# A two-layer block at 256 tokens: the first layer's work before its gathers put in another order

## The reference, cut to what matters

```python
# first layer: x is 1 x 256 x 1024
h = rmsnorm(x, norm1_gain)
aq, ak, av, mq, mk, mv, mi, mf, mo, gate_a, gate_m = split_columns(h @ w_in)
aq = partial_rope(rmsnorm(aq, q_norm_gain), positions)      # 16 heads of 64
ak = partial_rope(rmsnorm(ak, k_norm_gain), positions)      # 2 heads of 64
att_b = sliding_window_attention(aq, ak, av, sinks) @ w_branch_attn
hm = mlstm_chunkwise(mq, mk, mv, i_pre, f_pre)              # 8 heads, values of 128
hm = rmsnorm(hm, ml_out_norm_gain) * sigmoid(mo)
mixed = sigmoid(gate_a) * att_b + sigmoid(gate_m) * (hm @ w_branch_mlstm)
x = x + mixed @ w_out
x = x + peer_ffn(rmsnorm(x, norm2_gain), ...)
# peer_ffn: query projection, key scores, top 16 per head, 128 experts per token
# gathered by index (a down and an up row of 1024 each), softmax gate times gelu
# second layer, untouched: stick-breaking attention, HGRN2, a gated feed-forward
```

## Time and profile before

| | |
|---|---|
| median of 3 runs | 1484.26 us (1481.1 to 1486.63) |
| the profiled execution's own time | 1486.09 us |
| its span | 1484.3 us |
| PE busy | 1242.8 us (84%) |
| DVE busy | 725.6 us (49%) |
| ACT busy | 570.9 us (38%) |
| POOL busy | 819.7 us (55%) |
| mean granted TensorE clock | 0.93 of full speed |

### The profile page before, as it was taken

One profiled execution on the slowest core, in us unless ns is written; L12 is line 12 of the kernel. 1 busy time (PEld: TensorE's weight loads), 2 busy tenths in 40 slices (PEclk: granted clock), 3 DMA queues, 4 the chain that ended last, 5 costly groups with the idle time before them and its releaser, 6 DMA issues.

```text
span 1484.3 us, 16729 instructions
## 1 busy us (share of the span) xinstructions
PE 1242.8 (84%) x6460; PEld 902.9 (61%) x6460; DVE 725.6 (49%) x1423; ACT 570.9 (38%) x1220; POOL 819.7 (55%) x503
## 2 busy tenths in 40 slices
PE   5788879958668877787788878778899899999998
PEld 5787769858643333333333333333499899999997
DVE  3256310164567585858576766754467723311111
ACT  4345753122422232222233222322566546544442
POOL 5535437235565545544545454454286647698885
PEclk9889979979789989999989998999999999999999
DMA  6523323244079999999999999999754334455551
GB/s 193 171 96 100 99 86 113 68 132 142 29 304 426 425 426 424 425 425 426 425 425 426 424 426 426 426 425 426 285 166 160 114 110 147 162 184 194 181 189 57
DMA packets 136160, 381.91 MB, mean 257 GB/s; under 512 B 8208, under 2 KB 95376, under 8 KB 103312
## 3 DMA queue, kind: packets, MB, share of 16 engines
q0 software_dynamic: 36864, 268.45, 43.1%
q1 hardware_dynamic: 97776, 112.27, 23.0%
q10 hardware_dynamic: 1440, 0.11, 0.1%
HBM read 379.76 MB, written 1.05 MB: 257 GB/s over the span
## 4 chain that ended last, share of the span: by engine, by line
PE 50%; DMA 30%; DVE 10%; ACT 6%; issue 2%; POOL 2%; ACTq 0%; another core or an unknown queue 0%; SPq 0%; DVEq 0%
DMA rows_w<-peer_rows_in,arena 29%; PE ps L641 29%; PE ps L823 8%; PE ps L990 4%; PE ps L652 2%; PE ps L942 2%; DVE rows_w L1669 1%; ACT arena L1074 1%; POOL rows_w L557 1%; ACT wgt L1168 1%; DVE am L1474 1%; DVE am L1473 1%; PE ps L897 1%; ACT w_hi L395 1%; PE ps L692 1%
## 5 line engine op out<-in xcount | busy, mean ns | idle before, releaser
L403 POOL TENSOR_TENSOR w_lo<-ring,w_hi 128x1024 fp32r<-128x1024 f32 x202 | 487.3, 2428 | 348.8 <-ACT w_hi L395 348.8
L823 PE MATMUL ps<-rows_w,diag 128*128 128x512 f32 x512 | 258.8, 652 | 66.0 <-ACT diag L1174 66.0
L823 PE MATMUL ps<-arena,diag 128*128 128x512 f32 x448 | 217.4, 641 | 61.8 <-ACT diag L1174 61.8
L395 ACT ACTIVATE w_hi<-ring 128x1024 fp32r<-128x1024 f32 x202 | 205.5, 1048 | 143.1 <-PE ps L641 103.7
L641 PE MATMUL ps<-hT_hi,w_hi 128*128 128x256 f32 x832 | 243.8, 293 | 6.8 <-DVE hT_lo L596 6.8
L557 POOL DMA_INDIRECT rows_w<-peer_rows_in,arena x128 | 166.6, 1301 | 148.4 <-PE ps L823 134.7
L641 PE MATMUL ps<-hT_lo,w_hi 128*128 128x256 f32 x832 | 240.1, 289 | 0.0
L641 PE MATMUL ps<-hT_hi,w_lo 128*128 128x256 f32 x832 | 239.8, 288 | 0.0
L823 PEld LDWEIGHTS ps<-rows_w,diag 128*128 128x128 f32 x512 | 102.4, 206 | 214.6 <-issue 118.8
L1669 DVE CUSTOM_DVE_ANT_0 rows_w<-rows_w,arena 128x1024 f32<-128x1024 f32 x128 | 156.2, 1225 | 125.1 <-DMA rows_w<-peer_rows_in,arena 123.4
L557 POOL DMA_INDIRECT arena<-peer_rows_in,arena x112 | 133.5, 1192 | 139.7 <-PE ps L823 122.0
(11 more groups left out here) (365 smaller groups left out, 1696.5 us busy)
## 6 DMA issues: line engine op xcount, KB each, us to landing
ring<-w_in_in SPq DMA_DIRECT2D x46, 1024.0 KB, 5.1
ring<-w_ffn_gate_in SPq DMA_DIRECT2D x11, 1024.0 KB, 5.2
ring<-w_ffn_up_in SPq DMA_DIRECT2D x11, 1024.0 KB, 5.1
ring<-w_ffn_down_in SPq DMA_DIRECT2D x11, 1024.0 KB, 5.0
ring<-w_out_in SPq DMA_DIRECT2D x8, 1024.0 KB, 6.1
ring<-w_branch_attn_in SPq DMA_DIRECT2D x2, 2048.0 KB, 8.9
ring<-w_branch_mlstm_in SPq DMA_DIRECT2D x4, 1024.0 KB, 6.3
ring<-peer_w_query_in SPq DMA_DIRECT2D x4, 1024.0 KB, 4.9
```

Of the source, the lines that this page charges most:

```text
L395: act.activation(w_hi[:, u // 2 % 2, t, 0:cols], raw_half(n, g)[:, t, 0:cols], ACT.Copy).then_inc(sem("hi_ready"), 1)
L403: pool.tensor_tensor(w_lo[:, u // 2 % 2, t, 0:cols], raw_half(n, g)[:, t, 0:cols], w_hi[:, u // 2 % 2, t, 0:cols].bitcast(F32), ALU.subtra ...
L823: ins = pe.matmul(acc[:, c, :], diag[:, p % 4, :], pick_row(p % TOPK, D + c * CW, CW), start=False, stop=True, skip_group_check=True)
```

## The change

It touches the first layer up to its gathers. The gather phase, the choice of the top 16 and the second layer have the same instructions as before, with some semaphores renamed.

1. **Start.** x comes by two transfers, one per token block, and SP issues the weights behind them without a wait. The norm runs per block (square, logarithm, exponential on ACT), written in half rows so that PE can turn each as it comes. ACT waits for the gain column alone, not for all ten small inputs. The first half begins once two `hT_lo` tiles are there (`fresh`).
2. **Order.** k/v and the narrow columns are the first two halves, q the next four. Gate rows follow half 3, their spread half 5. The q/k turns follow halves 9 and 11 and the attention starts behind half 11. The root of q/k is an `Ln` and an `Exp` (`qk_root`) where it was a `Sqrt`.
3. **Attention** has six groups (two of eight heads on block 0, four of four heads on block 1) in nine steps. In step k PE does the values of group k-3, the transposes of group k-2 and the scores of group k. The output is split as it leaves PSUM, upper part on ACT, lower part on DVE (`att_low`).
4. **Memory** takes two heads a step in five steps. ACT squares each head's output with a running sum (`ssn`) as it empties the bank. `mo` leaves as a copy and one `Sigmoid` follows later. The masks of the weights are made on POOL.
5. **Branch.** `w_branch_attn` is split like all others. The turn of `hm` (`turn_hm`) stands behind its second half, and `hm` is made in 16 pieces of 128x128, each a fused multiply of raw output, root and gate.
6. **Gating** is done in the PSUM banks; the upper part of the sum leaves by ACT, the lower by DVE.
7. **Second norm.** PE turns the unscaled residual between the `w_out` halves (`turn_x2`), the gain goes into the split, and the row's root goes into the copy of the key scores and into `h2`. `sub_keys` and `n2row` are loaded earlier.

```diff
+ATT_GROUPS = ((0, 0, 8), (0, 8, 8), (1, 0, 4), (1, 4, 4), (1, 8, 4), (1, 12, 4))
+NATT = len(ATT_GROUPS)
+ABANK = (3, 2, 0, 1)
...
-        for c in range(2):
-            add_columns("aq", w1, AQ0 + c * CW)
         add_split("kv", w1[:, :, AK0:MQ0], w1[:, :, MI0:MO0])
-        for nm, c0, c1 in (("mq", MQ0, MK0), ("mk", MK0, MV0), ("mv", MV0, MI0), ("mo", MO0, GA0), ("gates", GA0, W1N)):
+        for nm, c0, c1 in (("aq", AQ0, AK0), ("mq", MQ0, MK0), ("mk", MK0, MV0), ("mv", MV0, MI0), ("mo", MO0, GA0), ("gates", GA0, W1N)):
             for c in range(c0, c1, CW):
...
-        v = wview(a["w_branch_attn"])
-        for c in range(2):
-            add("w_branch_attn", v[:, :, c * CW:(c + 1) * CW], "br_done")
-        NML = len(chunks)
-        for nm in ("w_branch_mlstm", "w_out"):
+        for nm in ("w_branch_attn", "w_branch_mlstm", "w_out"):
             for c in range(2):
...
-        GROUPS = NB * 4
-        att_steps = [("turn_qk", 0), ("turn_qk", 1)]
-        for g in range(GROUPS + 2):
-            att_steps.append(("attend", g))
-        att_steps += [("gate_rows", 0), ("spread", 0)] + [("memory", h) for h in range(MH + 1)]
-        plan1 = steps_after(halves_of(0, NW1 + 2), att_steps, 6)
+        halves1 = halves_of(0, NPEER)
+        N1H = 2 * NW1
+        TURN = 9
+        ATT0 = 11
+        MEM0 = ATT0 + NATT + 3
+        after1 = [[] for _ in halves1]
+        after1[3].append(("gate_rows", 0))
+        after1[5].append(("spread", 0))
+        after1[TURN].append(("turn_qk", 0))
+        after1[ATT0].append(("turn_qk", 1))
+        for k in range(NATT + 3):
+            after1[ATT0 + k].append(("attend", k))
+        for j in range(MH // 2 + 1):
+            after1[MEM0 + j].append(("memory", j))
+        after1[N1H + 1].append(("turn_hm", 0))
...
-            sp.dma_start(xres[:], a["x"].rearrange("(b p) n -> p b n", p=P)).then_inc(sem("x_loaded"), 16)
-            sp.wait_ge(sem("x_loaded"), 16)
-            sp.wait_ge(sem("small_loaded"), NSMALL * 16)
+            for b in range(NB):
+                sp.dma_start(xres[:, b, :], a["x"][b * P:(b + 1) * P, :]).then_inc(sem(f"x_loaded{b}"), 16)
             for n, (nm, views) in enumerate(chunks):
+                if n == NML:
+                    sp.wait_ge(sem("qk_turned"), NB)
+                    sp.wait_ge(sem("ml_qk"), MH // 2)
+                    sp.wait_ge(sem("num_evac"), MH)
+                    sp.dma_start(sk, a["sub_keys"]).then_inc(sem("sk_loaded"), 16)
+                if n == NO1:
+                    sp.wait_ge(sem("hm_tok"), MH)
+                    sp.dma_start(n2row, a["n2row"]).then_inc(sem("sk_loaded"), 16)
                 if n == NPEER:
-                    sp.wait_ge(sem("x2_ready"), 4)
-                    sp.dma_start(sk, a["sub_keys"]).then_inc(sem("sk_loaded"), 16)
-                    sp.dma_start(n2row, a["n2row"]).then_inc(sem("sk_loaded"), 16)
...
+                if k >= 3:
+                    b, h0, n = ATT_GROUPS[k - 3]
+                    pe.wait_ge(sem("probsT"), k - 2)
+                    if k >= 4:
+                        pe.wait_ge(sem("att_split"), k - 3)
+                    for i in range(2):
+                        for kb in range(b + 1):
+                            v = p1[:, kb, AV0 + h0 // 8 * AD:AV0 + (h0 // 8 + 1) * AD]
+                            moving = pt[:, 4 * kb + i:4 * kb + 4:2, :] if b else pt[:, i::2, :]
+                            ins = pe.matmul(ps[i * AD:(i + 1) * AD, 3, 0:n * AD], v, moving, start=(kb == 0), stop=(kb == b))
+                    ins.then_inc(sem("att_done"), 1)
...
+            def turn_x2(i):
+                pe.wait_ge(sem("x2_ready"), i + 1)
+                for t in (2 * i, 2 * i + 1):
+                    for b in range(NB):
+                        ins = pe.transpose(ps[:, 4 + i, (t % 2) * S + b * P:(t % 2) * S + (b + 1) * P], xres[:, b, t * P:(t + 1) * P], ident[:])
+                ins.then_inc(sem("in_turned"), 1)
...
+            do = {"turn_qk": turn_qk, "attend": attend, "gate_rows": gate_rows, "spread": spread, "memory": memory, "turn_hm": turn_hm}
...
+                    k = i - N1H
+                    if k:
+                        pe.wait_ge(sem("p1_evac"), N1H + k - 3)
+                    else:
+                        pe.wait_ge(sem("att_split"), NATT)
+                    split_half(n, g, False, ps[:, ABANK[k], :], attT_hi, attT_lo)
+                for what, k in after1[i]:
+                    do[what](k)
+            for k, (n, g) in enumerate(halves_of(NML, NO1)):
+                split_half(n, g, False, ps[:, 4 + k, :], hmT_hi, hmT_lo, fresh=None if k else LOW_HM)
+            for i, (n, g) in enumerate(halves_of(NO1, NQUERY)):
+                split_half(n, g, True, ps[:, ABANK[i], :], mixT_hi, mixT_lo, 0)
+                if i:
+                    turn_x2(i - 1)
+            turn_x2(3)
...
+            act.dma_start(gcol[:], a["gcol"]).then_inc(sem("gain_loaded"), 16)
...
+            act.preload_act_table_set(LOG_EXP)
+            act.wait_ge(sem("ident_ready"), 1)
+            for b in range(NB):
+                act.wait_ge(sem(f"x_loaded{b}"), 16)
+                link(act.activation(xn1[:, b, :], xres[:, b, :], ACT.Square, accum_out=ss[:, b:b + 1]))
+                link(act.activation(ms[:, b:b + 1], ss[:, b:b + 1], ACT.Ln, scale=1.0 / D, bias=eps_col[:, 0:1]))
+                act.activation(rr[:, b:b + 1], ms[:, b:b + 1], ACT.Exp, scale=-0.5).then_inc(sem("r_ready"), 1)
+            upper_parts(act, 0, 0)
+            act.wait_ge(sem("gain_loaded"), 16)
+            for t in range(KT):
...
+            def qk_root(b):
+                act.wait_ge(sem("qk_ms"), b + 1)
+                link(act.activation(hst[:, 1, :], hst[:, 0, :], ACT.Ln))
+                act.activation(hst[:, 2, :], hst[:, 1, :], ACT.Exp, scale=-0.5).then_inc(sem("qk_root"), 1)
...
+                    act.activation(hraw[:, :, h, :], bank, ACT.Copy)
+                    for b in range(NB):
+                        ins = act.activation(hjunk, bank[:, b, 0:MV], ACT.Square, accum_out=ssn[:, b, h:h + 1])
+                        link(ins)
+                    act.sem_inc(sem("num_evac"), 1)
...
+            for part in range(3):
+                act1[6 + part].append((spread, part))
+            act1[8].append((qk_root, 0))
+            act1[10].append((qk_root, 1))
+            act1[TURN].append((turn_qk, 0))
+            act1[ATT0].append((turn_qk, 1))
+            for k in range(NATT + 3):
+                act1[ATT0 + k].append((attend, k))
+            act1[MEM0 - 1].append((mo_gate, 0))
+            for j in range(1, MH // 2 + 1):
+                act1[MEM0 + j].append((memory, j))
+            for i, (n, g) in enumerate(halves1[0:N1H]):
+                leave1(n, g)
+                upper_parts(act, *halves1[i + 2])
+                for part, k in act1[i]:
+                    part(k)
...
+            def upper_mix1(k):
+                act.wait_ge(sem("mixed_sum"), k + 1)
+                act.activation(mixT_hi[:, 2 * k:2 * k + 2, :], ps[:, 4 + k, :].rearrange("p (a b) -> p a b", a=2), ACT.Copy).then_inc(sem("mixed_hi"), 1)
...
+                dve.tensor_tensor(attT_lo[:, t, b * P:(b + 1) * P], ps[:, 3, 0:n * AD].rearrange("p (a b) -> p a b", b=P),
+                                  attT_hi[:, t, b * P:(b + 1) * P].bitcast(F32), ALU.subtract).then_inc(sem("att_split"), 1)
...
-            for b in range(NB):
-                link(dve.tensor_tensor(hs[:, b, :, :], hraw[:, b, :, 0:MV], den[:, 1, b, :].unsqueeze(2).broadcast_to([P, MH, MV]), ALU.mult))
-            link(dve.tensor_tensor(hsq, hs, hs, ALU.mult))
-            link(dve.tensor_reduce(den[:, 0, :, :], hsq, AX, ALU.add))
-            dve.tensor_scalar(den[:, 1, :, :], den[:, 0, :, :], 1.0 / MV, EPS, ALU.mult, ALU.add).then_inc(sem("hm_ms"), 1)
+            link(dve.tensor_tensor(den[:, 2, :, :], den[:, 1, :, :], den[:, 1, :, :], ALU.mult))
+            dve.tensor_tensor(den[:, 3, :, :], den[:, 2, :, :], ssn[:], ALU.mult).then_inc(sem("hm_var"), 1)
             dve.wait_ge(sem("hm_root"), 1)
-            link(dve.reciprocal(den[:, 0, :, :], den[:, 2, :, :]))
-            for b in range(NB):
-                link(dve.tensor_tensor(hs[:, b, :, :], hs[:, b, :, :], den[:, 0, b, :].unsqueeze(2).broadcast_to([P, MH, MV]), ALU.mult))
-            dve.tensor_tensor(hs, hs, mo.rearrange("p b (h v) -> p b h v", h=MH), ALU.mult).then_inc(sem("hm_tok"), 1)
+            dve.wait_ge(sem("mo_ready"), 1)
+            link(dve.tensor_tensor(den[:, 0, :, :], den[:, 1, :, :], den[:, 2, :, :], ALU.mult))
+            for h in range(MH):
+                for b in range(NB):
+                    ins = dve.scalar_tensor_tensor(out=hs[:, b, h, :], in0=hraw[:, b, h, 0:MV], scalar=den[:, 0, b, h:h + 1],
+                                                   in1=mo[:, b, h * MV:(h + 1) * MV], op0=ALU.mult, op1=ALU.mult)
+                ins.then_inc(sem("hm_tok"), 1)
...
```

(4 more changed lines are left out.)

788 lines of the change are left out of this document (402 added, 386 removed).

## The result

The changed kernel takes 1411.52 us (median of 4 runs, 1410.46 to 1415.46) against 1483.38 us before: a ratio of 0.9519 (95% interval 0.9492 to 0.9545). The forecast was 1427 in a range of 1406 to 1448. The profiled execution took 1412.28 us, its span is 1410.4 us, 73.9 shorter than before; the forecast took 57.7 off. The time is almost to the microsecond that of rival B, so the first question is whether B's reason is the right one.

The account below looks back on a forecast made before the run. Gathers bound 651.1 us and PE the 417.8 behind them, both untouched; ahead of 415.40 PE is the bound with holes, and savings there pass on. Seven terms sum to -57.7 us, 1484.3 to 1426.6, said as 1427, range 1406 to 1448.

Parts of the forecast that it names:

- rival B: POOL's subtractions hardly delay the q/k chain, term 2 losing 14.7 us of stalls: 1412, with `hm` in time 1407; chance 0.24.
- Start: From kernel start to the first projection half: it begins at 14.9 us instead of 20.02, -5.1 us.
- The port: Ahead of the gathers, a DVE operation on SBUF operands that meets POOL waits up to one POOL instruction, 2.4 us.
- term 2: q and k, up to the first attention scores: +14.2 us, with PE stalls of 10.4 and 10.5 for rotated q.
- term 4: Gates and memory: waits of 6.4 and 3.4 us go, memory in pairs has the same matmuls; -13.2 us.
- Attention: Attention stretch: 78.4 us against 96.67, one half of it moved, waits 14.2 down to 2; -12.3 us.
- rival C: The loop of ACT and DVE sets the step in attention and memory: 18 us more, 1445; chance 0.22.
- `hm`: Attention branch and `hm`: 32.5 us against 51.7, with a PE wait of 5 for `hm`; -19.2 us.
- Second norm: From the end of `w_out` to the first gather: 29.4 us in place of 43.85, -14.5 us.
- D: Ahead of the first gather, DVE waits on POOL make the kernel slower than before: 1499 us with 30 more; chance 0.02.
- E: The gather phase takes back what was won ahead of it, so nothing comes of the change: 1484 us; chance 0.02.
- A: The sum of all terms ahead of the first gather holds: between 1418 and 1436 us; chance 0.50.

## Why the prediction was right, and where it was 16 us off

**What bounds it, and that time passes on.** Right: gathers and remainder kept their length to 0.2 us, in this kernel; in those tried, from the first gather to the end of the span, between 1065.6 and 1069.1 us.

**Start.** Right in the number, 14.8 for 14.9, and by luck in part: the squares began at 7.78 and not by 6.5, and the turns ended at 13.8 for 13.0, but the first half was then ready within 1.0 us, not 1.9. The load of the weights, which I had taken into the bounds, is worth 1 us of the 5.

**The port.** Right as a mechanism, shown by holding GpSimd back: 11.9 us of the 19.2. The Trainium skill's page "SBUF — State Buffer", section "Who interferes with whom", says that a VectorE instruction with two SBUF inputs contends with a GpSimd one that reads SBUF, that copies can enter modes that contend too, and that the later of the two waits for the whole of the other. The trace agrees for `tensor_tensor` and, in the later kernels, for the 128x128 copies (L1556 and L1557, 2.3 to 3.3 us for 0.22). The price of the stalls was 1.7 too high. The working of the second one does not add up: from the root at 110.4 to the turn at 123.7 are 13.3 us, where 4.8 and 2.8 subtractions give 11.5; the trace has 12.5.

**Halves behind a stop (term 2).** This is the first mis-sized part. I let half 0 run at 7.7 and the halves around gates and turns at 7.2 and more, and put the end of half 9 at 87.1. It was 82.67 in this trace, but 87.1 and 87.2 in two others. 4.4 us of the 16.4 by which the first gather came earlier than forecast are that draw, and should have stood in the range as a term of both signs. Half 10 and the turns gave another 1.3.

**Memory (term 4).** The step of the sum that was wrong in kind: "Memory in pairs has the same matmuls". It has, but two heads side by side take the time of one. 3.1 us of the 4.3 by which the term was too small are shown for that.

**Attention.** Right in kind: 1.8 us of waits left, 2 forecast, and a step of 8.5 us. The loop I feared in rival C did not set the step. Depth alone is about half of the gain.

**`hm`.** Right nearly to the number: ready 19.2 us behind half 25 (254.3 in the trace), 18.5 forecast, and a wait of 4.8 for 5. The 16 multiplies took 12.68 us, of which 3.5 are their own by the estimate of the prediction:

```profile
241.64 12.68 DVE L1625 SCALAR_TENSOR_TENSOR arena<-arena,den 128x128 f32<-128x128 f32 x16
```

**Second norm.** Too small by 1.3: the first query half ran at 6.0 and not 7.2, since PE hardly stops ahead of it (0.3 us).

**The rivals.** B is refuted though its number came out. Had I only compared times, I would have chosen it. C, D and E did not happen. A's waits came true but not its time: 1411.5 lies outside A's own 1418 to 1436, and inside the full range only because that reached down to B's low end. That the range held is luck in this sense: two terms missed for reasons that were in no rival, the draw of the first halves and the memory pairs.

## What to carry to other kernels

When two engines lock each other for whole instructions, price a chain by the number of its instructions and by what the other engine does at that time, not by its length: 4.8 us of work took 4.8, 10.6, 12.5 and 21.7 us here. Moving such a chain earlier can put it beside a busier neighbour; three places gave the same time. And when a forecast agrees with the clock, look whether its waits are in the trace before its reason is believed.
